# Gate-and-up products of the first chunk in other PSUM banks, the next unit ahead of the transposes, and the last step interleaved, in two chained transformer blocks

## The reference

```python
D_MODEL, SEQ, D_FF_2, CONV_WIDTH = 1024, 256, 2816, 3      # D_FF of the first block is 2816 too

def _swiglu(x, w_gate_up, w_down):                         # every FFN, in the first block with modulation around it
    a, b = jnp.split(x @ w_gate_up, 2, axis=-1)
    return (jax.nn.silu(a) * b) @ w_down

def _short_conv(x, w_in, conv_w, w_out):
    b_gate, c_gate, u = jnp.split(x @ w_in, 3, axis=-1)
    v = c_gate * u
    conv = lax.conv_general_dilated(
        v, conv_w[:, None, :], window_strides=(1,), padding=[(CONV_WIDTH - 1, 0)],
        dimension_numbers=("NWC", "WIO", "NWC"), feature_group_count=D_MODEL)
    return (b_gate * conv) @ w_out

def second_block(x, ...):
    h = x
    for layer in range(2):
        h = h + 0.5 * _swiglu(_rmsnorm(h, ffn_norm[layer, 0]), ...)
        hn = _rmsnorm(h, mix_norm[layer])
        h = h + (_short_conv(hn, ...) if layer < 1 else _nsa(hn, ...))
        h = h + 0.5 * _swiglu(_rmsnorm(h, ffn_norm[layer, 1]), ...)
        ...
    return h
```

## Time and profile before

| | before |
|---|---|
| median of 3 runs | 1614.5 us |
| lowest and highest of them | 1607.8 and 1615.29 us |
| the profiled execution's own time | 1612.2 us |
| its span, first to last instruction | 1610.2 us |
| TensorE busy | 1483.9 us (92%) |
| VectorE busy | 851.7 us (53%) |
| ScalarE busy | 690.7 us (43%) |
| mean granted TensorE clock | 0.967 of full speed |

### The profile page before, as it was taken

How to read it: one execution, slowest core, us unless ns; L and a number is a source line. 1 busy time by engine, 2 the same in 40 slices (tenths; PEclk the granted TensorE clock), 3 DMA queues, 4 the chain that set the end, 5 groups by cost and what they waited for, 6 DMA issues and landing times.

```text
span 1610.2 us, 17994 instructions
## 1 busy us (share of the span) xinstructions
PE 1483.9 (92%) x6942; PEld 1178.8 (73%) x6942; DVE 851.7 (53%) x1024; ACT 690.7 (43%) x865; POOL 34.2 (2%) x52
## 2 busy tenths in 40 slices
PE   4889988989999999999999999979999968899998
PEld 2546766678887788877778887767888854678886
DVE  1556764645545545554854445565444547555543
ACT  2344444343333544443444443564444446453442
POOL 0010000000000000000000000100000010000000
PEclk9998999989999999999999999989999968999999
DMA  8553664636554556545545555455555430056552
GB/s 313 183 190 131 213 206 151 214 118 197 182 184 155 185 188 201 183 133 181 180 160 184 187 188 173 137 173 167 185 187 188 150 105 1 27 172 194 182 185 77
DMA packets 187879, 270.09 MB, mean 168 GB/s; under 512 B 8350, under 2 KB 134118, under 8 KB 187816
## 3 DMA queue, kind: packets, MB, share of 16 engines
q1 hardware_dynamic: 186448, 267.01, 50.5%
q10 hardware_dynamic: 1208, 1.94, 0.3%
q0 software_dynamic: 160, 0.26, 0.2%
HBM read 268.15 MB, written 1.05 MB: 167 GB/s over the span
## 4 chain that ended last, share of the span: by engine, by line
PE 81%; DVE 8%; ACT 5%; DMA 3%; issue 3%; POOL 0%; SPq 0%; POOLq 0%; ACTq 0%; DVEq 0%
PE bank L1591 24%; PE bank L1593 24%; PE bank L1592 24%; DVE w_lo_ring L1150 2%; PE bank L1621 2%; ACT w_hi_ring L854 2%; PE bank L1693 1%; PE bank L1722 1%; DMA raw_ring<-in_w_in_dram 1%; DMA arena<-in_w_mod_dram 1%; PE bank L1775 1%; DVE arena L1446 1%; DMA raw_ring<-in_w_out_dram 1%; PE bank L1851 1%; DVE arena L1430 1%
## 5 line engine op out<-in xcount | busy, mean ns | idle before, releaser
L1150 DVE TENSOR_TENSOR w_lo_ring<-raw_ring,w_hi_ring 128x2048 fp32r<-128x2048 f32 x231 | 525.2, 2277 | 464.6 <-ACT w_hi_ring L1106 345.3
L1591 PE MATMUL bank<-w_hi_ring,h_hi 128*128 128x512 f32 (+2 forms) x1392 | 557.3, 400 | 18.6 <-DVE w_lo_ring L1150 11.0
L1593 PE MATMUL bank<-w_hi_ring,h_lo 128*128 128x512 f32 (+2 forms) x1392 | 545.0, 392 | 0.0
L1592 PE MATMUL bank<-w_lo_ring,h_hi 128*128 128x512 f32 (+2 forms) x1392 | 544.6, 391 | 0.0
L1106 ACT ACTIVATE w_hi_ring<-raw_ring 128x2048 fp32r<-128x2048 f32 x158 | 302.6, 1915 | 313.3 <-PE bank L1593 311.1
L1591 PEld LDWEIGHTS bank<-w_hi_ring,h_hi 128*128 128x128 f32 x1392 | 265.5, 191 | 87.5 <-issue 24.6
L1593 PEld LDWEIGHTS bank<-w_hi_ring,h_lo 128*128 128x128 f32 x1392 | 265.0, 190 | 56.3
L1592 PEld LDWEIGHTS bank<-w_lo_ring,h_hi 128*128 128x128 f32 x1392 | 265.8, 191 | 50.6
L1591 PE MATMUL bank<-w_hi_ring,f_hi 128*128 128x512 f32 (+1 forms) x456 | 177.6, 390 | 7.5 <-DVE f_lo L1549 7.5
L854 ACT ACTIVATE w_hi_ring<-raw_ring 128x2048 fp32r<-128x2048 f32 (+1 forms) x73 | 136.4, 1878 | 101.2 <-PE bank L1593 50.7
L1593 PE MATMUL bank<-w_hi_ring,f_lo 128*128 128x512 f32 (+1 forms) x456 | 177.0, 388 | 0.0
(11 more groups left out here) (230 smaller groups left out, 840.8 us busy)
## 6 DMA issues: line engine op xcount, KB each, us to landing
raw_ring<-in_ffn_w_gate_up_dram SPq DMA_DIRECT2D x176, 512.0 KB
raw_ring<-in_ffn_w_down_dram SPq DMA_DIRECT2D x44, 1024.0 KB
raw_ring<-in_w_in_dram SPq DMA_DIRECT2D x22, 1024.0 KB
raw_ring<-in_w_gate_up_dram SPq DMA_DIRECT2D x44, 512.0 KB
raw_ring<-in_w_mod_dram SPq DMA_DIRECT2D x18, 1024.0 KB
raw_ring<-in_w_down_dram SPq DMA_DIRECT2D x11, 1024.0 KB
raw_ring<-in_conv_w_in_dram SPq DMA_DIRECT2D x16, 512.0 KB
arena<-in_w_mod_dram SPq DMA_DIRECT2D x6, 1024.0 KB, 15.7
```

Of the source, the lines that this page charges most:

```text
L1150: dve.tensor_tensor(w_lo[:, u % RING, 0:words], raw[:, r % RING, 0:words], w_hi[:, u % RING, 0:words].bitcast(F32), ALU.subtract).then_inc ...
L1591: pe.matmul(dst, hi, whi, start=start, stop=False)
L1592: pe.matmul(dst, hi, wlo, start=False, stop=False)
L1593: return pe.matmul(dst, lo, whi, start=False, stop=stop)
```

## The change

Four things change in the list and in TensorE's program; no instruction is added or taken away, and no transfer moves.

1. Chunk 0 of each FFN goes into another pair of banks (`FIRST_PAIR`: banks 4 and 5, or 2 and 3), and the first unit of chunk 1 is issued ahead of the transposes of chunk 0.
2. In the last step of each FFN the transposes of chunk 10 stand between the two halves of the `down_product` of chunk 9.
3. In the convolution mixer the chunks alternate between two pairs of banks, each chunk's transposes (`gt`) stand behind the first unit of what comes next, and the four `conv` groups on VectorE come earlier.
4. With the pair of chunk 0, the wait for a free pair ahead of `gu` changes: f3 now waits for pair 1 where it waited for pair 0, and f1 waits for three updates of `x`.

```diff
+FIRST_PAIR = (2, 1, 2, 1, 2)
...
-    begin_glu("cv", 3)
-    for j in range(4):
-        add("glu", j=j, unit=len(units) - (0 if j else 2))
-        if j:
-            units.extend([("cv", j, 0), ("cv", j, 1)])
+    begin_glu("cv", 3)
     conv = [[dict(kind="conv", g=g)] for g in range(4)]
-    part("cb", 0, 0, 2, [conv[0]])
-    part("cb", 0, 1, 2, [evac("cb", 0), conv[1]])
-    part("cb", 1, 0, 2, [conv[2]])
-    plan.extend(tgroup("cb", 4)[:2] + conv[3])
+    glu_t = [dict(kind="gt", j=j) for j in range(4)]
+    add("then split", unit=len(units) - 2)
+    add("gp", j=0, half=1, unit=len(units) - 1)
+    for j in range(1, 4):
+        for half in range(2):
+            add("gp", j=j, half=half, unit=len(units))
+            units.append(("cv", j, half))
+            if half == 0:
+                plan.append(glu_t[j - 1])
+                plan.extend(conv[j - 2] if j > 1 else [])
+    part("cb", 0, 0, 2, [glu_t[3:], conv[2]])
+    part("cb", 0, 1, 2, [evac("cb", 0), conv[3]])
+    part("cb", 1, 0, 2)
+    plan.extend(tgroup("cb", 4)[:2])
...
-                    if item["sub"] == 0:
-                        free_pairs(item, (0,))
-                    ins = glu_unit(item["unit"], 0, item["need"], kks=kks)
+                    if item["sub"] == 0 and item["pair"] < 2:
+                        free_pairs(item, (item["pair"],))
+                    if item["sub"] == 0 and item["frees"] is not None:
+                        pe.wait_ge(sem("x_ready"), 4 * xu[2] - 4 + item["frees"])
+                    ins = glu_unit(item["unit"], 0, item["need"], kks=kks, pair=item["pair"])
...
+                        if jb == 0:
+                            glu_unit(u + 1, 1, item["need"], pair=FIRST_PAIR[f]).then_inc(sem("unit_used"), 1)
+                            return
+                        glu_unit(u, 0, None, two).then_inc(sem("unit_used"), 1)
+                        if jb == 1:
+                            glu_transposes(item["tg"], item["gi"])
+                        glu_unit(u + 1, 1, None, two).then_inc(sem("unit_used"), 1)
                         u += 2
...
+                        for kk in range(2):
+                            for tt in range(TT):
+                                for nb in range(2):
+                                    ins = down_product(u, fb, kk, nb, tt, jb == 1 and kk == 0, False)
+                            if jb == NJ - 1 and kk == 0:
+                                glu_transposes(item["tg"] + jb, item["gi"] + jb)
+                        ins.then_inc(sem("unit_used"), 1)
+                        if jb < NJ - 1:
+                            glu_transposes(item["tg"] + jb, item["gi"] + jb, two, 0 if i is None else i)
```

More of the change, by code:

```diff
@@ L94, in tgroup, with ffn @@
         return [dict(a, kind="tp", stage=stage, g=g) for g in range(n)]
-    def ffn(f, stage, norm, then=None, begun=False):
-        body = add("ffn", f=f, stage=stage, norm=norm, unit=len(units) - (2 if begun else 0), begun=begun)
+    def ffn(f, stage, norm, then=None):
+        body = add("ffn", f=f, stage=stage, norm=norm, unit=len(units) - 2)
         for j in range(NJ + 1):
-            if j < NJ and not (begun and j == 0):
+            if 0 < j < NJ:
                 units.extend([(stage, j, 0), (stage, j, 1)])
@@ L111, in norm_rest, with begin_glu @@
         add("square")
-    def begin_glu(stage, norm):
+    def begin_glu(stage, norm, pair=0, inside=None, frees=None):
         u = len(units)
         units.extend([(stage, 0, 0), (stage, 0, 1)])
-        add("gu", unit=u, sub=0)
-        norm_rest(norm)
-        add("gu", unit=u, sub=1)
+        add("gu", unit=u, sub=0, pair=pair, frees=frees)
+        norm_rest(norm) if inside is None else plan.extend(inside)
+        add("gu", unit=u, sub=1, pair=pair)
     def lin_out(stage, then, inside=()):
@@ L325, in make_plan @@
     part("cm", 1, 1, 2, [evac("cm", 1)])
[L326 to L329, removed]
+    begin_glu("f3", 6, FIRST_PAIR[3], [dict(kind="tp", stage="kc", g=0), dict(kind="tp", stage="hc", g=0, c=1)])
     add("cmp", s=1)
-    ffn(3, "f3", 6, then=7, begun=True)
+    ffn(3, "f3", 6, then=7)
     part("qg", 0, 0, 2, inside=[tgroup("norm", 4, norm=7)[2:] + [dict(kind="square")], []])
@@ L356, in make_plan @@
             split(item["unit"] + RING)
-        if item["kind"] == "glu":
-            split(item["unit"] + 1 + RING)
+        if item["kind"] == "gp":
+            split(item["unit"] + RING)
         if item["kind"] == "ffn":
@@ L422, in make_plan @@
                 unit_raw[u] = transfer("unit", u)
-        if k == "glu":
-            item["tg"], item["gi"] = number("tg"), number("gi")
-        if k in ("gu", "ffn", "glu", "nsa"):
+        if k == "gp" and item["half"]:
+            item["gi"] = number("gi")
+        if k == "gt":
+            item["tg"], item["gi"] = number("tg"), count["gi"] - 1
+        if k in ("gu", "ffn", "nsa"):
             item["pairs_before"] = [count.get(f"pair{q}", 0) for q in range(2)]
@@ L1076, in _ @@
                                    ACT.Copy).then_inc(sem("xp_hi_ready"), 1)
[L1077 to L1078 removed]
+                if k == "gp" and item["half"]:
+                    j = item["j"]
+                    if j == 0:
                         act.wait_ge(sem("rstd_ready"), 4)
[L1080 removed]
+                    act.wait_ge(sem("unit_used"), item["unit"] + 1)
                     for tt in range(TT):
[L1082 removed]
+                        act.activation(glu_s[:, tt, :], bank[2 * (j % 2) + tt][:, 0:GC], ACT.Copy, scale=rstd[:, tt:tt + 1])\
                            .then_inc(sem("sg_ready"), 1)
+                if k == "gt":
                     act.wait_ge(sem("t_done"), item["tg"] + 1)
@@ L1519, in _ @@
                             tick(ins) if hh < 3 else ins.then_inc(sem("v_bd_ready"), 1)
-                if k == "glu":
-                    gi = item["gi"]
-                    if item["j"] == 0:
+                if k == "gp" and item["half"]:
+                    gi, j = item["gi"], item["j"]
+                    if j == 0:
                         dve.memset(v_t[:, :, 0:2], 0.0).then_inc(sem("v_t_ready"), 1)
@@ L1593, in three, with glu_unit @@
                 return pe.matmul(dst, lo, whi, start=False, stop=stop)
-            def glu_unit(u, half_, need=None, two=lambda a: 0, kks=range(4)):
+            def glu_unit(u, half_, need=None, two=lambda a: 0, kks=range(4), pair=0):
                 pe.wait_ge(sem("raw_done"), u + 1 + two(3))
@@ L1603, in glu_unit @@
                     for tt in range(TT):
-                        ins = three(bank[tt][:, :], h_hi[:, kt, tt * P:(tt + 1) * P], h_lo[:, kt, tt * P:(tt + 1) * P],
+                        ins = three(bank[2 * pair + tt][:, :], h_hi[:, kt, tt * P:(tt + 1) * P], h_lo[:, kt, tt * P:(tt + 1) * P],
                                     wv[0], wv[1], kt == 0, kt == KT - 1)
```

74 lines of the change are left out of this document (28 added, 46 removed).

## The result

| | before | after |
|---|---|---|
| median | 1613.0 us (4 runs, 1607.8 to 1615.29) | 1587.1 us (4 runs, 1584.45 to 1587.99) |
| span of the profiled execution | 1610.2 us | 1586.1 us |
| mean granted clock | 0.967 | 0.964 |

The ratio is 0.984, with a 95% interval of 0.9825 to 0.9861: the change makes the kernel 1.6% faster. The forecast was 1585.0.

The account below looks back on a forecast made before the run. TensorE's work plus its idle waits bound the kernel (busy 1483.9 of 1610.2 us). Gains of 27.8 us gave 1584.4 from the profiled 1612.2, or 1586.7 from the median 1614.5; it took 1585, range 1577 to 1595.

Parts of the forecast that it names:

- What an idle costs: On TensorE, an idle of this kind costs its own length plus 0.29 us (0.13 slower restart, 0.16 uncounted).
- Chunk 0, 8.1: At chunk 0 of each FFN, five waits on `glu_a` go, hidden beside chunk 1's first unit; gain 8.1 us.
- Last step, 8.2: At the end of each FFN, five waits on `f_lo` go, by a margin of 0.06 us; gain 8.2 us.
- rival B: In each FFN's last step `f_lo` is late again and the wait stays; 8.2 lost, 1592.6 us; chance 0.06.
- Mixer and its output product, 6.2 + 1.45 + 1.77 + 1.6: Mixer: four chunk waits gone (6.2 us), two output-product waits on `h_lo` cut (1.45, 1.77), slow clock behind them gone (1.6).
- f3, 0.5: Ahead of f3, `gu` no longer waits for the pair that ScalarE's line 1012 frees; gain 0.5 us.
- Rival A: In the mixer's output product VectorE stays late, so both waits and the slow clock stay; 1589.2 us; chance 0.12.
- Rival C: At chunk 1 of each FFN a wait for `w_lo_ring` replaces that for `glu_a`; 1592.5 us; chance 0.03.
- Rival D: Around the moved units, bank alternation drops TensorE's clock to 1.2 GHz; slower, 1683 us if all 23 fell; chance 0.02.
- whole of f0: In the first FFN, the granted clock is 1.00 throughout, given as evidence against a clock drop from bank cycling.
- The sum: Over the whole kernel, the gains of all terms add up to 27.8 us.

Follow-up runs that it names:

- minus_chunk0: The changed kernel with chunk 0 of each FFN as before (banks 0 and 1, transposes right behind its own products); 1598.44 us, ratio 0.9905.
- 18 of 24: The changed kernel with the last step's transposes behind 18 of the down product's 24 matmuls in place of 12; 1589.38 us, ratio 0.9844.
- minus_last: The changed kernel with the last step of each FFN as before (transposes of chunk 10 behind all 24 matmuls); 1595.96 us, ratio 0.988.
- 6 of 24: The changed kernel with the last step's transposes behind 6 of the down product's 24 matmuls in place of 12; 1586.86 us, ratio 0.983.
- conv_late: The changed kernel with the four convolution groups at their old places in VectorE's queue; 1593.36 us, ratio 0.9869.
- gn_late: The changed kernel with the gate projection's narrow matmuls behind the second chunk of queries, in a wait of TensorE; 1580.89 us, ratio 0.9794.

## Why the prediction was right

*What an idle costs.* Idle plus 0.29 is confirmed by the mixer's 11.36, and its part of 0.13 by the 16.94 at f2 of minus_chunk0. It is the price of a wait in the list, not of one under 0.4: the 0.27 at 18 of 24 cost 0.24 to 0.34.

*Chunk 0, 8.1.* Right in place and size; undoing it brings the five waits back. What the step missed is the clock: it read from the earlier trace rows that a single idle of up to 2.09 has no slow matmuls behind it. In two further kernels with the same wait it had, worth 1.4 more. The term is 8.1 to 9.5. Why the clock fell behind this wait in two kernels and not in the third stays open; that the kernel before was profiled in the cheaper case is luck for the sum.

*Last step, 8.2.* 8.1 by minus_last. The chain that the prediction named (`f_lo` behind the subtraction on VectorE, then 0.84) is the one in the trace. Its thin margin mattered less than rival B had it: 18 of 24 shows that missing by 0.27 costs about 0.3 an FFN, not the 1.65. At 6 of 24 nothing is lost either, so the place at 12 needed no exact fit. For rival B in full, with 8.2 lost, `f_lo` would have had to come well over a microsecond later.

*Mixer and its output product, 6.2 + 1.45 + 1.77 + 1.6.* 11.05 against 11.02. conv_late shows that the last three terms hang on where the convolution stands in VectorE's queue, and it brings the clock's fall back as well. The slow clock was there in both profiles that had the two waits (before, conv_late) and in none of the eleven others, so nothing here shows the case in which this 1.6 is missing. Rival A ended at one wait of 0.2 instead of two.

*f3, 0.5.* The wait had no row in the changed kernel and is back with 0.5 in minus_chunk0. Its share can't be read from the stretch, since kv+f3 differs by 0.7 between profiles of one kernel.

*Rival C*, the late weights, has no row. *Rival D*, the clock by bank cycling: over f1, and over the mixer, which alternates between pairs now, the changed kernel's windows read

```profile
530.00:702.00 172.00, 172.00 (x780) 142.17 (x779) 87.83 (x66) 72.86 (x64) 0.00 (x0) 1.00 0.61 195
722.00:795.00 73.00, 72.76 (x336) 59.83 (x335) 49.27 (x58) 31.45 (x27) 0.00 (x0) 1.00 0.60 191
```

at 1.00 throughout. (The prediction's "whole of f0" was read from 342 on; near the start of its stretch f0 has some slow matmuls left over from the stage ahead, in both kernels.) The Trainium skill (TensorE: Matmul & The Clock Gate, A second HAM failure mode: psum-queue depth-cycling) has a kernel whose clock oscillated when it cycled through banks; this trace doesn't show it.

*The sum.* 27.8 forecast; 28.0, 28.4 and 28.7 in the touched stretches of the three profiles; 25.9 between the medians. The stretches left alone differ from one execution of one kernel to the next (by 1.4 in the gates and by 10.6 at the start), together more than the 2 us between the forecast of 1585 and the median of 1587.1. That these 2 us are not more is therefore luck; the terms are what was confirmed.

## What to carry to other kernels

Price a removed wait in the stretch where it stood, between two instructions that both kernels have, and not by the time of the whole: here the six stretches together gave 28.0 to 28.7 us while whole executions of one kernel differed by 11. Stretches near a place where the clock had been low (f0, kv+f3) repeated less well than the others. A wait of 2 us may also carry a slow clock behind it, so removing it may be worth half as much again; here it did in two kernels of three. Narrow matmuls that nothing needs soon belong into a wait that is there anyway, with no wide ones behind them; but ask first what they were covering where they stood.

## What the hardware did that was not expected

TensorE's clock fell to 0.50 while TensorE was busy without a gap, among or right behind 48 matmuls of 48 columns. The distance between two of them went from 0.11 to 0.21 us, and 5 to 12 wide ones behind them took 0.43 instead of 0.23 each. It did so in all ten profiles with that order, at a place that moved by at least 20 matmuls, and in gn_late too, where the 48 stand elsewhere. Why it falls there is not shown. And the same wait of 2.1 us, at the same place in the same order of work, had slow matmuls behind it in two kernels and none in a third. The Trainium skill (the same page, What's actually happening) says of a kernel's start that how many matmuls run slow differs from run to run. The rows here show such a difference in the middle of a kernel, and a loss in windows in which TensorE is busy throughout.
